# The taps of GpSimd in a depthwise convolution: the multiply as a tensor operation with a broadcast weight

## The chip, the cores and the metric

The kernel runs on one core of a Trainium2 chip. The metric is the device time of one launch in microseconds (us). Three executions of the kernel before are given, and beside them one execution that was profiled.

## The reference

Two layers of a transformer block work on a sequence of 512 latent positions and a context of 256, 1024 channels wide, all in float32. The first layer mixes by neighbourhood attention (8 heads) beside a gated depthwise convolution of 31 taps over 512 channels; the second by a chunked mLSTM. Each layer ends in a SwiGLU. What the change touches is the convolution of the first layer:

```
u, gt = ...                       # two products of h with w_in, 512 channels each
glu = u * sigmoid(gt)
def depthwise_conv(x, w, b):      # w: [31, 512], one weight for each tap and channel
    y = conv(x, w, padding 15 on each side, one group for each channel)
    return y + b
conv_out = silu(layer_norm(depthwise_conv(glu, conv_w, conv_b), ln_g, ln_b))
out = concat([attention, conv_out]) @ w_out
```

## The kernel before, in words

Channels lie on the 128 partitions, positions along the columns. The 512 channels of the convolution are four blocks i = 0 to 3. For each block `glu_out` (L1134) writes the gated input to one of two buffers, `glu0` and `glu1` (block i uses i % 2), with latent and context side by side and zeros between them and around, so that one tap is a shift of the input by one column: a view of SPAN = 798 columns.

The 31 taps of a block are shared out between two engines. VectorE takes the first 18 (DVE_TAPS, `conv_steps` at L1113): one fused multiply and add each (L1120) into its own accumulator `convy[i]`. GpSimd takes the other 13 (POOL_TAPS, `pool_conv` at L378): the first tap is a multiply into `y2` (L388), each later one a multiply into `ptmp` (L392) and an add of `ptmp` to `y2` (L394), each waiting for the one ahead by the semaphore `s_pc`. The weight is one column of `small`, so a value for each partition. That is 13 multiplies and 12 adds for each block, 52 and 48 in all. `merge(i)` (L1127, the operation at L1132) on VectorE waits for both and adds `y2` to `convy[i]`. There is one `y2`, so the first multiply of the next block (L388) waits for the merge of the block ahead (`s_mrg`).

GpSimd also writes masked bias tables for the attention (`masks(hp)`, L352; operations at L367, L369 and L372), one set for each of four head pairs. Its order is written out by hand (L397 to L407): masks(0), block 0, six taps of block 1, masks(1), the rest of block 1, four taps of block 2, masks(2), the rest, four taps of block 3, masks(3), the rest. Much later, in the second layer, it has 16 multiplies at L416, whose two inputs are both broadcast views.

The attention runs in 24 steps U (six for each head pair), and in each of them the four other engines follow orders written out by hand. TensorE: scores (L1668, L1672), transposes of the probabilities (L1686), pieces of the remaining projections (L1643), attend (L1697), small products for the conditioning (L1546, L1553). ScalarE: exponentials (L728), copies of the transposed probabilities (L737). VectorE, for each U: `biased_max(U+1)` (L1162, which waits for the masks by `s_bx`), two or so taps, `normalise(U+1)` (L1178), splits of weights (L430), more taps, and in U = 2, 7, 12 and 18 a merge, then `attn_lo(U)` (L1186), which gates the next transposes. So what stands behind a merge in VectorE's queue is the attention itself.

```
            TAPS_AT = (4, 4) + 16 * (3,)
                conv_steps(taps - min(1 if w_a is not None else 2, taps))
                if U in (2, 7, 12, 18):
                    merge((2, 7, 12, 18).index(U))
```

After the last merge, TensorE sums the four blocks for the layer norm in U = 19 (L1731, L1732, which wait for `s_mrg` 4), the attention steps 19 to 23 end, and the output product of the first layer begins (L1597) at 409.65 us. All that follows (some 1560 us, mostly products at L445) depends on it.

Of the kernel before, what the change touches and what calls it, by code (L numbers as in the profile page):

```python
# [107 lines left out]
def program(nc, A, out):  # L108
    f32, f32r = mybir.dt.float32, mybir.dt.float32r
    ACT, ALU, AX = mybir.ActivationFunctionType, mybir.AluOpType, mybir.AxisListType  # L110
    ctx = ExitStack()
    with ctx:
# [3 lines left out]
        def sem(name):  # L116
            return ctx.enter_context(nc.semaphore(name))
# [27 lines left out]
        def sm(name, i, n=1):  # L145
            return small[:, SM[name][0] + i:SM[name][0] + i + n]
# [4 lines left out]
        def carve(base, at, *shape):  # L151
            n = int(np.prod(shape))
            v = base[:, at:at + n]
            if len(shape) == 2:
                v = v.rearrange("p (a b) -> p a b", a=shape[0])
            if len(shape) == 3:
                v = v.rearrange("p (a b c) -> p a b c", a=shape[0], b=shape[1])
            if len(shape) == 4:
                v = v.rearrange("p (a b c d) -> p a b c d", a=shape[0], b=shape[1], c=shape[2])
            return v, at + n  # L160
# [14 lines left out]
        SPAN = LAT + CTX + 30  # L175
# [3 lines left out]
        y2, at = carve(Xf, at, SPAN)  # L179
        ptmp, at = carve(Xf, at, SPAN)  # L180
# [101 lines left out]
        s_conv, s_pc, s_mrg = sem("conv_step"), sem("pool_conv_step"), sem("conv_merged")  # L282
# [27 lines left out]
        @block.sync  # L310
        def _(sp):
            trig = CN["cos"][0]
            scr_w = scr[:, 0:8192].rearrange("p (a n) -> p a n", a=8)
            sp.dma_start(small[:], A["small"]).then_inc(s_small, 16)
            for i in range(4):
                sp.dma_start(X[:, 2 * i:2 * i + 2], A["xT"][:, 2 * i:2 * i + 2]).then_inc(s_xp[i], 16)
            sp.dma_start(const[:, 0:trig], A["const"][:, 0:trig]).then_inc(s_const, 16)
            for i in range(4):
                if i >= 2:
                    sp.wait_ge(s_adm, 4 * (i - 1))  # L320
                for c in range(2):
                    to = 4 * (i % 2) + 2 * c
                    src = A["ada"][8 * c + 2 * i:8 * c + 2 * i + 2].rearrange("a p n -> p a n")
                    sp.dma_start(scr_w[:, to:to + 2], src).then_inc(s_ada0[i], 16)
                if i == 0:
                    for r in range(2):
                        sp.dma_start(raw[:, r], A["w"][r]).then_inc(s_raw[r], 16)
            sp.dma_start(const[:, trig:NCN], A["const"][:, trig:NCN]).then_inc(s_const, 16)
            for p in range(2, 20):
                sp.wait_ge(s_lo, p - 1)  # L330
                sp.dma_start(raw[:, p % 2], A["w"][AB_ROWS[p]]).then_inc(s_raw[p % 2], 16)
            with sp.Fori(10, NR // 2) as i:
                r = sp.snap(2 * i)
                for j in range(2):
                    src = A["w"][bass.ds(sp.snap(r + j), 1)].rearrange("a p n -> p (a n)")
                    sp.wait_ge(s_lo, r + (j - 1))
                    sp.dma_start(raw[:, j], src).then_inc(s_raw[j], 16)


        @block.gpsimd  # L340
        def _(pool):
            pool.wait_ge(s_h, 8)
            for v in (glu0, glu1, bx0, bx1):
                nc.gpsimd.memset(v, 0.0).then_inc(s_zero, 1)
            for c in range(16):

                src = bass.AP(A["rpb"].tensor, 7 * 384 + 7 * 48 + 15 - c, [[384, 8], [-48, 64], [1, 32]])
                pool.dma_start(braw[8 * c:8 * c + 8].rearrange("p a h k -> p (a h) k"), src).then_inc(s_braw, 16)
            pool.wait_ge(s_braw, 256)
            pool.wait_ge(s_zero, 4)  # L350

            def masks(hp):  # L352

                if hp:
                    pool.wait_ge(s_mx, 8 * hp)
                for h in range(2):
                    H, b = 2 * hp + h, bx[h]
                    for kind, first, k0, k1, kb0, kn, keep in (
                            (0, 256, 8, 16, 8, 8, "low"), (0, 320, 16, 24, 16, 16, None), (0, 320, 24, 32, 16, 16, "high"),
                            (1, 256, 0, 16, 0, 16, "low"), (1, 384, 16, 32, 16, 16, "high"),  # L360
                            (2, 256, 0, 8, 0, 16, "low"), (2, 256, 8, 16, 0, 16, None), (2, 384, 16, 24, 16, 8, "high")):

                        dst = b[:, BX[kind] + first:BX[kind] + first + 8 * kn].rearrange("p (a k) -> p a k", a=8)
                        dst = dst[:, :, k0 - kb0:k1 - kb0]
                        src = braw[:, :, H, k0:k1]
                        if keep is None:
                            i = nc.gpsimd.tensor_copy(dst, src)  # L367
                        elif keep == "low":
                            i = nc.gpsimd.affine_select(out=dst, in_=src, compare_op=ALU.is_ge, fill=-BIG, base=8 * k0 + 7,  # L369
                                                        pattern=[[0, 8], [8, k1 - k0]], channel_multiplier=-1)  # L370
                        else:
                            i = nc.gpsimd.affine_select(out=dst, in_=src, compare_op=ALU.is_ge, fill=-BIG, base=120 - 8 * k0,  # L372
                                                        pattern=[[0, 8], [-8, k1 - k0]], channel_multiplier=1)
                        i.then_inc(s_bx, 1)

            steps = [0]

            def pool_conv(i, j0, j1):  # L378

                src = glus[i % 2]  # L380
                for j in range(j0, j1):
                    tap = DVE_TAPS + j
                    w = sm("conv_w", TAPS * i + tap)
                    if j == 0:
                        pool.wait_ge(s_gf[1], (3, 5, 7, 9)[i])
                        if i:
                            pool.wait_ge(s_mrg, i)
                        nc.gpsimd.tensor_scalar(y2, src[:, tap:tap + SPAN], w, None, ALU.mult).then_inc(s_pc, 1)  # L388
                        steps[0] += 1
                        continue  # L390
                    pool.wait_ge(s_pc, steps[0])
                    nc.gpsimd.tensor_scalar(ptmp, src[:, tap:tap + SPAN], w, None, ALU.mult).then_inc(s_pc, 1)  # L392
                    pool.wait_ge(s_pc, steps[0] + 1)
                    nc.gpsimd.tensor_tensor(y2, y2, ptmp, ALU.add).then_inc(s_pc, 1)  # L394
                    steps[0] += 2

            masks(0)  # L397
            pool_conv(0, 0, POOL_TAPS)
            pool_conv(1, 0, 6)
            masks(1)  # L400
            pool_conv(1, 6, POOL_TAPS)
            pool_conv(2, 0, 4)
            masks(2)
            pool_conv(2, 4, POOL_TAPS)
            pool_conv(3, 0, 4)
            masks(3)
            pool_conv(3, 4, POOL_TAPS)  # L407

            pool.wait_ge(s_g2, GD_END)
            for n in range(16):  # L410
                H, d = n // 2, n % 2
                if n:
                    pool.wait_ge(s_R, n)
                row = nrow[0:48, d, None, :].to_broadcast([48, CH, 128])
                pick = ident[0:48, H:32:8][:, :, None].to_broadcast([48, CH, 128])
                nc.gpsimd.tensor_tensor(rsel[0:48].rearrange("p (c i) -> p c i", c=CH), row, pick, ALU.mult)\  # L416
                    .then_inc(s_rs2, 1)
# [1566 lines left out]
```

## Time and profile before

| | |
|---|---|
| runs | 1965.87, 1968.57, 1973.45 us; median 1968.57 |
| the profiled execution | 1973.65 us, its span 1971.8 us |
| PE busy | 1768.8 us (90% of the span) |
| DVE busy | 844.2 us (43%) |
| ACT busy | 559.9 us (28%) |
| POOL busy | 276.9 us (14%), x204 |
| PE's mean granted clock | 0.921 |

Busy shares are averages over a span in which the stages differ much: GpSimd's work lies nearly all between 59 us and 373 us, in the attention and convolution of the first layer, and in slices 4 to 8 of the 40 (0.2 to 0.4 of a millisecond) it is 90% busy or more. POOL is GpSimd, DVE VectorE, ACT ScalarE, PE TensorE.

### The profile page before, as it was taken

What the parts mean: (1) busy time and instruction counts of PE and PEld (TensorE: products, weight loads), DVE (VectorE), ACT (ScalarE), POOL (GpSimd) and SP (SyncE); (2) the same over time, 40 slices, a digit from 0 to 9 for tenths busy, and PEclk for the clock granted to TensorE, in tenths of its full rate; (3) what the DMA queues carried; (4) which work ended last, traced back from release to release, by engine and by line L of the source; (5) the groups of instructions that cost most, each with busy time, mean ns of one, the idle gap of its engine ahead of it and who ended that gap; (6) DMA issues with size and microseconds to landing.
All of it is one profiled execution on the core that took longest, in us unless ns stands there. A gap on an engine that the chain in (4) does not pass through costs nothing.

```text
span 1971.8 us, 26385 instructions
## 1 busy us (share of the span) xinstructions
PE 1768.8 (90%) x10440; PEld 1459.5 (74%) x10440; DVE 844.2 (43%) x1217; ACT 559.9 (28%) x901; POOL 276.9 (14%) x204
## 2 busy tenths in 40 slices
PE   5989897588999999999999468988989989999997
PEld 4877675367888888888888467666757768787886
DVE  4377686634422222222223525556545443333333
ACT  3334454242321112211222302332333232122131
POOL 0396999500000000000000000000000000000000
PEclk8999898689999999999999759898869999999999
DMA  7623332022113421233215301001002323323333
GB/s 301 76 75 108 101 125 97 1 86 64 44 63 105 148 89 63 59 138 134 63 64 192 120 0 43 22 33 32 22 11 75 128 75 96 95 88 94 96 96 106
DMA packets 47314, 168.99 MB, mean 86 GB/s; under 512 B 5392, under 2 KB 5648, under 8 KB 47120
## 3 DMA queue, kind: packets, MB, share of 16 engines
q1 hardware_dynamic: 31408, 115.47, 18.4%
q10 hardware_dynamic: 15072, 51.53, 7.3%
q0 software_dynamic: 768, 1.08, 0.7%
q8 instruction: 45, 0.74, 0.2%
q14 instruction: 21, 0.17, 0.0%
HBM read 163.83 MB, written 4.19 MB: 85 GB/s over the span
## 4 chain that ended last, share of the span: by engine, by line
PE 78%; DVE 8%; POOL 6%; ACT 3%; issue 2%; DMA 2%; SPq 0%; ACTq 0%; DVEq 0%; POOLq 0%
PE PS L445 57%; PE PS L1643 5%; POOL X L392 3%; PE PS L1537 3%; POOL X L394 2%; PE PS L1546 2%; PE PS L1767 2%; PE PS L1869 2%; DMA scr<-in_ada 2%; PE PS L1868 1%; DVE scr L1416 1%; PE PS L1843 1%; PE PS L1597 1%; DVE w_lo L430 1%; DVE h_lo L963 1%
## 5 line engine op out<-in xcount | busy, mean ns | idle before, releaser
L445 PE MATMUL PS<-h_hi,w_hi 128*128 128x512 f32 (+1 forms) x1296 | 401.0, 364 | 3.7 <-DVE w_lo L430 3.2
L445 PE MATMUL PS<-h_lo,w_hi 128*128 128x512 f32 (+1 forms) x1296 | 394.0, 358 | 0.0
L445 PE MATMUL PS<-h_hi,w_lo 128*128 128x512 f32 (+1 forms) x1296 | 393.8, 358 | 0.0
L430 DVE TENSOR_TENSOR w_lo<-raw,w_hi 128x1024 fp32r<-128x1024 f32 x196 | 240.9, 1231 | 280.3 <-ACT w_hi L425 267.3
L425 ACT ACTIVATE w_hi<-raw 128x1024 fp32r<-128x1024 f32 x196 | 206.2, 1052 | 299.5 <-PE PS L445 244.1
L445 PEld LDWEIGHTS PS<-h_hi,w_hi 128*128 128x128 f32 x1296 | 217.7, 192 | 47.8 <-DVE w_lo L430 5.6
L445 PEld LDWEIGHTS PS<-h_lo,w_hi 128*128 128x128 f32 x1296 | 216.8, 191 | 37.1
L445 PEld LDWEIGHTS PS<-h_hi,w_lo 128*128 128x128 f32 x1296 | 215.5, 190 | 37.3
L445 PE MATMUL PS<-c_hi,w_hi 128*128 128x512 f32 (+1 forms) x688 | 215.9, 367 | 24.7 <-DVE c_lo L1009 18.7
L445 PE MATMUL PS<-c_lo,w_hi 128*128 128x512 f32 (+1 forms) x688 | 213.4, 363 | 0.0
L445 PE MATMUL PS<-c_hi,w_lo 128*128 128x512 f32 (+1 forms) x688 | 212.4, 362 | 0.0
L995 DVE SCALAR_TENSOR_TENSOR X<-PS,mod,X 128x512 f32 (+1 forms) x96 | 60.6, 659 | 279.5 <-PE PS L445 271.5
L416 POOL TENSOR_TENSOR scr<-adaw,const 48x512 f32<-48x512 f32 x16 | 16.7, 1043 | 1069.4 <-DVE adaw L1348 808.3
L445 PEld LDWEIGHTS PS<-c_hi,w_hi 128*128 128x128 f32 x688 | 115.9, 193 | 49.1 <-issue 26.2
L445 PEld LDWEIGHTS PS<-c_hi,w_lo 128*128 128x128 f32 x688 | 116.8, 193 | 20.8
L445 PEld LDWEIGHTS PS<-c_lo,w_hi 128*128 128x128 f32 x688 | 116.5, 193 | 19.9
L392 POOL TENSOR_SCALAR X<-X,small 128x798 f32<-128x798 f32 x48 | 126.7, 2639 | 4.4
L1007 DVE TENSOR_TENSOR scr<-PS,scr 128x768 f32<-128x768 f32 (+1 forms) x44 | 36.3, 824 | 170.8 <-PE PS L445 170.8
L552 ACT ACTIVATE c_hi<-scr 128x768 f32 (+3 forms) x44 | 32.5, 739 | 267.6 <-DVE scr L1007 267.6
L1120 DVE SCALAR_TENSOR_TENSOR c_early<-X,small,c_early 128x798 f32<-128x798 f32 x68 | 97.6, 1436 | 1.1
L549 ACT ACTIVATE scr<-PS 128x768 f32<-128x768 f32 (+1 forms) x44 | 31.1, 706 | 191.8 <-PE PS L445 185.8
L394 POOL TENSOR_TENSOR X<-X 128x798 f32<-128x798 f32 x48 | 83.3, 1736 | 4.0
(259 smaller groups left out, 2055.6 us busy)
## 6 DMA issues: line engine op xcount, KB each, us to landing
raw<-in_w SPq DMA_DIRECT2D x196, 512.0 KB, 3.4
scr<-in_ada ACTq DMA_DIRECT2D x48, 512.0 KB, 5.7
adaw<-in_ada ACTq DMA_DIRECT2D x32, 512.0 KB, 4.3
scr<-in_ada SPq DMA_DIRECT2D x8, 1024.0 KB, 10.6
X<-in_xT SPq DMA_DIRECT2D x4, 768.0 KB, 6.8
X<-in_xT ACTq DMA_DIRECT2D x1, 3072.0 KB, 9.9
x_spill<-X ACTq DMA_DIRECT2D x1, 2048.0 KB, 9.3
X<-x_spill ACTq DMA_DIRECT2D x1, 2048.0 KB, 8.6
```

The source lines that it names most:

```text
L392: nc.gpsimd.tensor_scalar(ptmp, src[:, tap:tap + SPAN], w, None, ALU.mult).then_inc(s_pc, 1)
L394: nc.gpsimd.tensor_tensor(y2, y2, ptmp, ALU.add).then_inc(s_pc, 1)
L425: nc.scalar.activation(w_hi[:, j], raw[:, j].rearrange("p (k n) -> p k n", k=KT), ACT.Copy).then_inc(s_hi, 1)
L430: nc.vector.tensor_tensor(w_lo[:, j], raw[:, j].rearrange("p (k n) -> p k n", k=KT), w_hi[:, j].bitcast(f32), ALU.subtract).then_inc(s_lo, 1)
L445: last = nc.tensor.matmul(G[j][:, a:b], w[:, j, k], m[:, k, a:b], start=(n == 1), stop=(n == 3 * k_tiles))
L995: i = V.scalar_tensor_tensor(out=xs, in0=G[j][:, a:b], scalar=gv, in1=xs, op0=ALU.mult, op1=ALU.add)
L1120: V.scalar_tensor_tensor(out=y, in0=src, scalar=w, in1=y, op0=ALU.mult, op1=ALU.add)\
L1537: last = MM(G[j][:, a:b], x[:, j, k], m[:, k, a:b], start=(k == 0 and n == 0), stop=(k == KT - 1 and n == 2))
L1546: last = MM(PS[g:g + 32, bank, 128 * q:128 * q + 128], sT[:, k], w[:, 128 * k:128 * k + 128], start=(k < 4), stop=(k >= 4))
L1643: last = MM(dst[:, a:b], w[:, p % 2, k], m[:, k, a:b], start=(k == 0 and n == 0), stop=(k == KT - 1 and n == 2))
L1767: last = MM(PS[:, 4, 32 * c:32 * c + 32], x[:, k, 128 * c:128 * c + 128], w[:, k], start=(k == 0 and n == 0), stop=(k == KT - 1 and n == 2))
L1869: last = MM(dst, Pm[:, n % 2, cc], vaug[:, h, c], start=False, stop=True)
```

## The change

The two multiplies of `pool_conv`, at L388 and L392, become tensor operations: the second input is the same column of `small`, now a view that repeats it along 798 columns. The adds, the order, the waits, the masks and the split of taps stay.

```
--- before.py
+++ after.py
@@ -385,11 +385,11 @@
                         pool.wait_ge(s_gf[1], (3, 5, 7, 9)[i])
                         if i:
                             pool.wait_ge(s_mrg, i)
-                        nc.gpsimd.tensor_scalar(y2, src[:, tap:tap + SPAN], w, None, ALU.mult).then_inc(s_pc, 1)
+                        nc.gpsimd.tensor_tensor(y2, src[:, tap:tap + SPAN], w.to_broadcast([128, SPAN]), ALU.mult).then_inc(s_pc, 1)
                         steps[0] += 1
                         continue
                     pool.wait_ge(s_pc, steps[0])
-                    nc.gpsimd.tensor_scalar(ptmp, src[:, tap:tap + SPAN], w, None, ALU.mult).then_inc(s_pc, 1)
+                    nc.gpsimd.tensor_tensor(ptmp, src[:, tap:tap + SPAN], w.to_broadcast([128, SPAN]), ALU.mult).then_inc(s_pc, 1)
                     pool.wait_ge(s_pc, steps[0] + 1)
                     nc.gpsimd.tensor_tensor(y2, y2, ptmp, ALU.add).then_inc(s_pc, 1)
                     steps[0] += 2
```

## Rows read from the trace of the kernel before

**Rows 1.** Profile page, part 4: shares of the chain that ended last, by engine.
```profile
PE 78%; DVE 8%; POOL 6%; ACT 3%; issue 2%; DMA 2%; SPq 0%; ACTq 0%; DVEq 0%; POOLq 0%
```

**Rows 2.** The chain that ended last, 244 to 373 us: start us, us, what.
```profile
244.18 0.99 DVE c_early L1132
245.33 2.30 POOL X L388
...
309.86 2.31 POOL X L388
...
371.22 1.61 POOL X L394
```

**Rows 3.** Groups of instructions by line, GpSimd: busy us, mean ns, idle before.
```profile
L392 POOL TENSOR_SCALAR X<-X,small 128x798 f32<-128x798 f32 x48 | 126.7, 2639 | 4.4
L394 POOL TENSOR_TENSOR X<-X 128x798 f32<-128x798 f32 x48 | 83.3, 1736 | 4.0
...
L388 POOL TENSOR_SCALAR X<-X,small 128x798 f32<-128x798 f32 x4 | 9.2, 2295 | 21.2 <-DVE c_early L1132 21.2
```

**Rows 4.** Single lines: min/median/max ns, first and last start us.
```profile
L392 POOL TENSOR_SCALAR X<-X,small x48: 2284/2359/3959, 107.2 to 368.9; 128x798 f32<-128x798 f32 x48
...
L394 POOL TENSOR_TENSOR X<-X x48: 1595/1608/2392, 109.5 to 371.2; 128x798 f32<-128x798 f32 x48
...
L416 POOL TENSOR_TENSOR scr<-adaw,const x16: 1041/1042/1047, 1181.1 to 1457.9; 48x512 f32<-48x512 f32 x16
```

**Rows 5.** GpSimd's instructions in order of time, 180 to 212 us.
```profile
182.80 2.29 POOL L388 TENSOR_SCALAR X<-X,small 128x798 f32<-128x798 f32 x1 [17.65 <-DVE c_early L1132]
...
207.64 0.29 POOL L369 TENSOR_SCALAR_AFFINE_SELECT scr<-X 128x64 f32<-128x64 f32 x1
...
211.22 0.29 POOL L372 TENSOR_SCALAR_AFFINE_SELECT c_early<-X 128x64 f32<-128x64 f32 x1
```

**Rows 6.** VectorE's instructions in order of time, idle time before them in brackets.
```profile
211.64 0.62 DVE L1162 CUSTOM_DVE_ANT_0 scr<-PS,c_early 128x448 f32<-128x448 f32 x1 [9.22 <-issue]
...
297.96 1.04 DVE L1120 SCALAR_TENSOR_TENSOR c_early<-X,small,c_early 128x798 f32<-128x798 f32 x1
308.69 0.99 DVE L1132 TENSOR_TENSOR c_early<-c_early,X 128x798 f32<-128x798 f32 x1 [9.70 <-POOL X L394]
...
362.33 2.59 DVE L1178 TENSOR_SCALAR scr<-scr 128x512 f32<-128x512 f32 x2
372.93 0.99 DVE L1132 TENSOR_TENSOR c_early<-c_early,X 128x798 f32<-128x798 f32 x1 [8.01 <-POOL X L394]
```

**Rows 7.** TensorE at 215.79 us, with its idle time and releaser.
```profile
215.79 1.12 PE L1697 MATMUL PS<-scr 128*64 128x128 f32 x8 [6.54 <-ACT scr L737]
```

**Rows 8.** Windows, TensorE alone: stretch, length, busy (x), granted clock, DMA share, GB/s.
```profile
215.80:222.40 6.60, 6.60 (x53) 0.50 0.53 193
...
309.80:315.40 5.60, 5.54 (x22) 0.54 0.02 4
```

**Rows 9.** Windows of blocks 1, 2, 3, multiplies of L392 alone: POOL busy (x), clock.
```profile
182.00:244.00 62.00, 31.18 (x12) 0.92 0.33 110
245.00:309.00 64.00, 31.25 (x12) 0.97 0.38 129
309.00:373.00 64.00, 29.83 (x12) 0.74 0.15 50
```

**Rows 10.** The same windows, adds of L394 alone.
```profile
182.00:244.00 62.00, 20.87 (x12) 0.92 0.33 110
245.00:309.00 64.00, 20.47 (x12) 0.97 0.38 129
309.00:373.00 64.00, 20.46 (x12) 0.74 0.15 50
```

**Rows 11.** VectorE's taps at L1120: min/median/max ns, first and last start us.
```profile
L1120 DVE SCALAR_TENSOR_TENSOR c_early<-X,small,c_early x68: 1035/1051/2428, 106.2 to 356.6; 128x798 f32<-128x798 f32 x68
```

More of the change, by code:

```diff
@@ L387, in pool_conv @@
                             pool.wait_ge(s_mrg, i)
-                        nc.gpsimd.tensor_scalar(y2, src[:, tap:tap + SPAN], w, None, ALU.mult).then_inc(s_pc, 1)
+                        nc.gpsimd.tensor_tensor(y2, src[:, tap:tap + SPAN], w.to_broadcast([128, SPAN]), ALU.mult).then_inc(s_pc, 1)
                         steps[0] += 1
@@ L391, in pool_conv @@
                     pool.wait_ge(s_pc, steps[0])
-                    nc.gpsimd.tensor_scalar(ptmp, src[:, tap:tap + SPAN], w, None, ALU.mult).then_inc(s_pc, 1)
+                    nc.gpsimd.tensor_tensor(ptmp, src[:, tap:tap + SPAN], w.to_broadcast([128, SPAN]), ALU.mult).then_inc(s_pc, 1)
                     pool.wait_ge(s_pc, steps[0] + 1)
```

## The prediction

> **What bounds the kernel now.** I read the chain that ended last first, because GpSimd's 14% of the span says nothing about it. The chain gives GpSimd 6% of the span [rows 1], and in order of time this share is one piece: from the merge of block 1 at 244.18 us to the last add at 371.22 us the chain runs almost without a break through GpSimd's multiplies and adds [rows 2]. Ahead of and behind that stretch it runs through TensorE. So the question is what is late there, and what would be late next.
>
> Then VectorE's instructions in order of time, for what waits for GpSimd. There are three such places [rows 6]. (a) `biased_max(6)` at 211.64, idle 9.22 us before it: it waits for masks(1), which GpSimd reaches only after six taps of block 1 and finishes at 211.22 + 0.29 = 211.5 [rows 5]. (b) The merge of block 2 at 308.69: VectorE was ready at 297.96 + 1.04 = 299.0 and waited 9.70. (c) The merge of block 3 at 372.93, ready at 362.33 + 2.59 = 364.9, waited 8.01. The merges of blocks 0 and 1 don't wait; at block 0 it is GpSimd that idles 17.65 us [rows 5].
>
> **What one multiply costs after.** As it is, one takes 2.295 us undisturbed (L388, mean) and 2.639 on average at L392; the add, a tensor operation with the same 798 columns on the same engine, takes 1.736 on average [rows 3], 1.595 at least [rows 4]. The open price is that of a tensor multiply with one input that repeats a single column. The trace has one: L416 multiplies two broadcast views, 512 columns, in 1.042 us, with a spread of 6 ns [rows 4]. That is 2.04 ns a column, against 1.600/798 = 2.00 for the add and 2.295/798 = 2.88 for the scalar form. So neither the multiply nor the zero step costs extra, and I price the new multiply as the add: 798 x 2.04 = 1.62 us undisturbed, and in each stretch the mean of the adds there. L416 runs on 48 partitions only; should the time depend on them the price is open, so the bounds are 1.60 us (the add) below and 3.96 us (the longest multiply now, [rows 4]) above. I take the value near the add, as the same opcode on the same shape.
>
> The trace thus has the two-input form faster than the one-input form, 1.60 against 2.30 us. The Trainium skill, GPSIMD Engine Reference, Engine selection, says the reverse: two-input elementwise operations are about twice as slow as on VectorE because both inputs share one read port, one-input ones run at roughly line rate. By that rule this edit could only lose, and the slower rival below would be the forecast; the trace disagrees with it at the scalar form.
>
> **The sum, wait by wait.** Block 0: 12 multiplies and the first get shorter, some 13 us in all. Worth nothing: the idle time of 17.65 us before block 1 [rows 5] grows instead, since merge(0) comes from VectorE's own order. If that cover were gone it would be 13 us.
>
> (a) Up to masks(1), GpSimd runs L388 (2.29 to about 1.65, saves 0.6) and five multiplies. In block 1 twelve L392 take 31.18 us [rows 9] and twelve adds 20.87 [rows 10], so one multiply saves (31.18 - 20.87)/12 = 0.86, five 4.3. Masks(1) ends 4.9 to 5.1 us earlier, at 206.5. `biased_max(6)` would have been free at about 205.5, so I count 5.1. TensorE's wait of 6.54 us behind it [rows 7] shrinks to about 1.4. That wait also costs a clock: after it the granted clock is 0.50 for 6.6 us [rows 8], so the 1.2 GHz level; the same work at full clock takes half, so 3.2 us more. Steps follow each other by TensorE there, so both count: **8.3 us**.
>
> Block 1: GpSimd saves 12 x 0.86 + 0.7 = 11 us and ends near 232, while VectorE comes to merge(1) at 244.18 - 8.3 = 235.9. It still doesn't wait, and block 2 starts 8.3 us earlier, near 237.0.
>
> (b) Block 2: multiplies 31.25 to 20.47 [rows 9, 10], 10.8, and 0.7 for the first: 11.5. Its last add ends at 308.6 - 8.3 - 11.5 = 288.8. VectorE is ready at 299.0 - 8.3 = 290.7, so the wait is gone and what is late next is the attention itself. merge(2) moves from 308.7 to 290.7, **18.0 us** in all.
>
> (c) Block 3: multiplies 29.83 to 20.46 [rows 9, 10], 9.4, and 0.7: 10.1. GpSimd ends at 372.8 - 18.0 - 10.1 = 344.7. VectorE's own arrival: 364.9 - 18.0 = 346.9, less the low-clock stretch after the wait of (b) (5.6 us at 0.54 [rows 8], so about 2.9) = 344.0. The two are level; merge(3) falls near 344.8 instead of 372.9, **28.1 us** in all.
>
> After merge(3) nothing changes: sums, last steps, output product and the 1560 us behind keep their lengths and shift. The L416 multiplies are untouched. No wait, DMA or buffer is added; the load of X behind merge(3) moves with it. Sum against the profiled execution: 1973.65 - 28.1 = 1945.5. That execution is 5.1 above the median of the runs shown, so the forecast for the median is 1968.57 - 28.1 = **1940.5 us**.
>
> **What is uncertain in it.** GpSimd's and VectorE's instructions slow each other while both run: L392 loses 0.34 us on average (2.639 - 2.295), the adds 0.14 (1.736 - 1.595, [rows 3, 4]), and VectorE's taps, 1.05 us at the median, reach 2.43 [rows 11]. In my sum the new multiply loses as little as an add. If it keeps more, its mean is 2.0 instead of 1.74, 0.26 more each: six before masks(1) 1.6 us; block 2 then ends at 288.8 + 1.6 + 13 x 0.26 = 293.8 where VectorE is ready at 292.3, 1.5; block 3 another 3.4; 6.5 in all, so a gain of 21.6. On the other side, with GpSimd's instructions shorter, VectorE is held for less each time: it could arrive at merge(3) some 3 us sooner and GpSimd too, for a gain of 33.
>
> **The rivals.** *Contention eats part* (chance 0.20): the new multiply is held as often as the old, mean 2.0 us; gain 21.6, so 1947. For it: both inputs now come from SBUF. Against: the adds have two and are held least. *More comes back* (0.17): VectorE's holds shrink, gain 33, 1935.5. *The form was not what cost* (0.04): multiplying takes its 2.3 us in any form, no change, 1968.6. Against: the multiplies at L416. *Slower: the repeated column is fetched in a pass of its own* (0.04). The multiply then takes two passes of the add, 3.2 us, plus 0.3 of holding: 3.5, 0.9 more than now. Masks(1) comes 5.4 later; block 1 ends 13 x 0.9 = 11.7 later, at 254.7, past VectorE's 249.6, so GpSimd then bounds every block: 10.5 + 11.7 + 11.7 = 34 us, 2002.5. It decides from a mean of 2.64 us on. Here too L416 speaks against it, where both inputs repeat. The rule of the Trainium skill named above (GPSIMD Engine Reference, Engine selection) points to this side. The forecast itself has 0.55.
>
> **How the numbers follow.** Something like 0.5% (10 us) is what a measurement of this kernel can tell from no change. The forecast, the contention case and the case of more all lie beyond it: 0.92 faster. Same 0.04, slower 0.04. The range takes in these three cases and the spread of the runs (about 3 below and 5 above the median): 1935.5 less 5 is 1930.5, 1947 plus 5 is 1952.
>
> **What the profile after should show.** L388 and L392 as TENSOR_TENSOR with a minimum near 1.61 us and a mean of 1.7 to 1.8, about 41 us less busy time on GpSimd; masks(1) ending near 206.5 and no low-clock stretch behind it; GpSimd idle some 31 us before block 1 about 5 before block 2 and 3 before block 3; the wait of merge(2) gone or under 1 us; merge(3) near 345 with a wait of 0 to 3 us; the output product beginning near 381.5; lengths behind it unchanged. I am wrong if the minimum of the multiply is not near the add's, if merge(2) still waits several us for L394, or if the stretch behind 409.65 changes its length.

## The result and the profile after

The change made the kernel slower: 1982.10 us median of 20 runs against 1972.92 of 20, ratio 1.0049, 95% interval 1.0038 to 1.0061. The profiled execution took 1980.02 us. I had forecast 1940.5.

The price of the multiply was right, and better than forecast. From the views of single lines of the kernel after (min/median/max ns):

```profile
L392 POOL TENSOR_TENSOR X<-X,small x48: 1507/2138/2580, 111.6 to 370.9; 128x798 f32<-128x798 f32 x48
...
L394 POOL TENSOR_TENSOR X<-X x48: 1595/2222/2662, 113.2 to 372.5; 128x798 f32<-128x798 f32 x48
...
L1120 DVE SCALAR_TENSOR_TENSOR c_early<-X,small,c_early x68: 1032/2184/2434, 106.4 to 372.6; 128x798 f32<-128x798 f32 x68
```

A multiply that nobody disturbs takes 1.51 us, less even than the add. But the medians tell the rest. The add, which was not touched, goes from 1.608 to 2.222 us, and VectorE's tap, not touched either, from 1.051 to 2.184 [rows 4, 11]. The medians have moved from the undisturbed to the disturbed value: each engine now holds up the other in more than half of these instructions. The groups by line on the page after (busy us, mean ns) say what that sums to:

```profile
L1120 DVE SCALAR_TENSOR_TENSOR c_early<-X,small,c_early 128x798 f32<-128x798 f32 x68 | 121.4, 1785 | 1.1
...
L394 POOL TENSOR_TENSOR X<-X 128x798 f32<-128x798 f32 x48 | 97.3, 2027 | 3.8
L392 POOL TENSOR_TENSOR X<-X,small 128x798 f32<-128x798 f32 x48 | 92.9, 1936 | 3.5
```

GpSimd's 96 instructions fall from 210.0 us [rows 3] to 190.2, and its busy time in all from 276.9 to 259.2, so 17.7 us where I had counted on 41. And VectorE pays: its taps take 121.4 us where they took 97.6 (68 at a mean of 1.436), its busy time rises by 38 us to 882.5. The chain that ended last shows who sets the end now (page after, part 4, by engine):

```profile
PE 77%; DVE 13%; ACT 3%; DMA 2%; issue 2%; POOL 1%; SPq 0%; ACTq 0%; DVEq 0%; POOLq 0%
```

GpSimd went from 6% to 1%, VectorE from 8% to 13% [rows 1]. In order of time the places of [rows 5, 6] look so (VectorE, then GpSimd, of the kernel after; idle time before the instruction in brackets):

```profile
189.44 0.98 DVE L1132 TENSOR_TENSOR c_early<-c_early,X 128x798 f32<-128x798 f32 x1
...
250.47 0.98 DVE L1132 TENSOR_TENSOR c_early<-c_early,X 128x798 f32<-128x798 f32 x1
...
312.99 0.98 DVE L1132 TENSOR_TENSOR c_early<-c_early,X 128x798 f32<-128x798 f32 x1
...
379.20 0.98 DVE L1132 TENSOR_TENSOR c_early<-c_early,X 128x798 f32<-128x798 f32 x1
```

```profile
190.57 1.52 POOL L388 TENSOR_TENSOR X<-X,small 128x798 f32<-128x798 f32 x1 [26.00 <-DVE c_early L1132]
251.59 1.52 POOL L388 TENSOR_TENSOR X<-X,small 128x798 f32<-128x798 f32 x1 [5.35 <-DVE c_early L1132]
314.11 1.52 POOL L388 TENSOR_TENSOR X<-X,small 128x798 f32<-128x798 f32 x1 [4.97 <-DVE c_early L1132]
```

No merge waits for GpSimd any more; GpSimd waits for every merge. The merges stand 7.8, 6.3, 4.3 and 6.3 us later than before (181.6, 244.2, 308.7, 372.9). The whole loss is there after block 0; blocks 1 to 3 take 189.8 us against 191.3.

How the two engines interlock is seen in block 0, where VectorE runs several taps in a row. Before, GpSimd has one scalar-form multiply and one tensor add in turn:

```profile
126.83 2.90 POOL L392 TENSOR_SCALAR X<-X,small 128x798 f32<-128x798 f32 x1
129.81 1.94 POOL L394 TENSOR_TENSOR X<-X 128x798 f32<-128x798 f32 x1
```

and VectorE beside it:

```profile
127.61 1.60 DVE L1120 SCALAR_TENSOR_TENSOR c_early<-X,small,c_early 128x798 f32<-128x798 f32 x1
...
129.24 1.05 DVE L1120 SCALAR_TENSOR_TENSOR c_early<-X,small,c_early 128x798 f32<-128x798 f32 x1
...
130.33 2.27 DVE L1120 SCALAR_TENSOR_TENSOR c_early<-X,small,c_early 128x798 f32<-128x798 f32 x1
```

The tap at 127.61 begins and ends inside the scalar-form multiply, at 1.60 us; the next takes its undisturbed 1.05; the one that meets the tensor add takes 2.27 and ends 0.85 us after the add. A pair on GpSimd lasts 5.0 us and three taps go by. After the change:

```profile
129.48 2.14 POOL L392 TENSOR_TENSOR X<-X,small 128x798 f32<-128x798 f32 x1
131.70 2.23 POOL L394 TENSOR_TENSOR X<-X 128x798 f32<-128x798 f32 x1
```

```profile
130.29 2.18 DVE L1120 SCALAR_TENSOR_TENSOR c_early<-X,small,c_early 128x798 f32<-128x798 f32 x1
...
132.50 2.27 DVE L1120 SCALAR_TENSOR_TENSOR c_early<-X,small,c_early 128x798 f32<-128x798 f32 x1
```

One tap for each tensor operation, strictly in turn: a pair lasts 4.5 us and two taps go by. GpSimd's pair is 10% shorter, and VectorE's tap a third longer (2.25 against 1.67 us).

### The profile page after: what moved, and what is told of

It reads as the page before. It is cut to its first block, busy times and chain, and to the rows that moved or that the text cites. A ratio compares the mean times of both kernels' runs of the same rounds, so it can differ in the third digit from the quotient of the medians.

```text
span 1978.2 us, 26385 instructions
## 1 busy us (share of the span) xinstructions
PE 1761.7 (89%) x10440; PEld 1453.8 (73%) x10440; DVE 882.5 (45%) x1217; ACT 560.2 (28%) x901; POOL 259.2 (13%) x204
## 4 chain that ended last, share of the span: by engine, by line
PE 77%; DVE 13%; ACT 3%; DMA 2%; issue 2%; POOL 1%; SPq 0%; ACTq 0%; DVEq 0%; POOLq 0%
PE PS L445 56%; PE PS L1643 5%; DVE c_early L1120 3%; PE PS L1537 3%; DMA scr<-in_ada 2%; PE PS L1546 2%; PE PS L1767 2%; PE PS L1869 2%; PE PS L1868 1%; DVE w_lo L430 1%; DVE scr L1416 1%; PE PS L1843 1%; DVE scr L1178 1%; PE PS L1697 1%; PE PS L1597 1%
## 5 line engine op out<-in xcount | busy, mean ns | idle before, releaser
L430 DVE TENSOR_TENSOR w_lo<-raw,w_hi 128x1024 fp32r<-128x1024 f32 x196 | 246.6, 1260 | 277.3 <-ACT w_hi L425 264.3
L1120 DVE SCALAR_TENSOR_TENSOR c_early<-X,small,c_early 128x798 f32<-128x798 f32 x68 | 121.4, 1785 | 1.1
L394 POOL TENSOR_TENSOR X<-X 128x798 f32<-128x798 f32 x48 | 97.3, 2027 | 3.8
L392 POOL TENSOR_TENSOR X<-X,small 128x798 f32<-128x798 f32 x48 | 92.9, 1936 | 3.5
## 6 DMA issues: line engine op xcount, KB each, us to landing
X<-in_xT ACTq DMA_DIRECT2D x1, 3072.0 KB, 10.1
```

The source lines that it names most:

```text
L392: nc.gpsimd.tensor_tensor(ptmp, src[:, tap:tap + SPAN], w.to_broadcast([128, SPAN]), ALU.mult).then_inc(s_pc, 1)
L430: nc.vector.tensor_tensor(w_lo[:, j], raw[:, j].rearrange("p (k n) -> p k n", k=KT), w_hi[:, j].bitcast(f32), ALU.subtract).then_inc(s_lo, 1)
L1120: V.scalar_tensor_tensor(out=y, in0=src, scalar=w, in1=y, op0=ALU.mult, op1=ALU.add)\
```

## The experiments

Theory H: a GpSimd operation with two inputs in SBUF (the tensor form) holds up a two-input VectorE instruction for nearly all its length, the scalar form for only a part. Rivals: W, that it is the reading of the repeated weight column; R, that a tap waits once for each GpSimd instruction whatever its form, so that shorter ones mean more waits.

### Which property of the operation holds VectorE up

**e1_swap**: the tensor multiply stays, the add becomes a scalar form.

```
-                    nc.gpsimd.tensor_tensor(y2, y2, ptmp, ALU.add).then_inc(s_pc, 1)
+                    nc.gpsimd.tensor_scalar(y2, ptmp, w, None, ALU.mult).then_inc(s_pc, 1)
```

> The multiplies of GpSimd are the tensor form with the repeated weight, as after the change, but its 48 adds are replaced by scalar-form multiplies (y2 = ptmp times weight), so its taps are not summed up. The mix of forms is thus that of before with the roles swapped. Theory H (a GpSimd tensor operation, with two inputs in SBUF, holds up a VectorE tap for all its length, the scalar form for only a part): VectorE's taps at L1120 fall back to the mean of before, 1.4 to 1.5 us, merge of block 0 near 182 us, time within 5 us of before. Rival W (it is the reading of the repeated weight column, next to VectorE's own reads of the weights, that holds VectorE up): taps stay at 1.7 to 1.8 us, merge of block 0 near 189 us.

**e2_full_operand**: the second input of L392 is 798 real columns.

```
-ptmp, src[:, tap:tap + SPAN], w.to_broadcast([128, SPAN]), ALU.mult
+ptmp, src[:, tap:tap + SPAN], src[:, tap:tap + SPAN], ALU.mult
```

> As after the change, but the second input of the 48 multiplies at L392 is the 798-column input itself (a square), not the repeated weight: its taps are left out of the result. Theory H: the same as after the change, taps at L1120 1.7 to 1.8 us on average, the multiply 1.5 to 1.6 us at least and about 1.95 on average, merge of block 0 near 189 us. Rival W: taps back at 1.4 to 1.5 us.

**e3_short_scalar**: the kernel before, L392 cut in length.

```
-nc.gpsimd.tensor_scalar(ptmp, src[:, tap:tap + SPAN], w, None, ALU.mult)
+nc.gpsimd.tensor_scalar(ptmp[:, 0:520], src[:, tap:tap + 520], w, None, ALU.mult)
```

> The kernel before, with the 48 scalar-form multiplies at L392 cut to 520 of 798 columns (the rest is left out of the result): one takes some 1.5 us undisturbed, as long as the tensor form after the change, so GpSimd's instructions come as densely. Theory H: the form decides, so in a pair of multiply and add VectorE still gets more than two taps through; taps at L1120 1.3 to 1.5 us on average, merge of block 0 near 182 us, and merges 2 and 3 come without a wait: 20 to 30 us faster than before. Rival R (a VectorE tap waits once for each GpSimd instruction, whatever its form, so shorter ones mean more waits): taps 1.7 to 1.8 us, merge of block 0 near 189 us, time like after.

**e4_all_scalar**: the kernel before with the edit of e1 to its adds.

> The kernel before with its 48 adds replaced by scalar-form multiplies (GpSimd's taps are not summed up): no tensor operation is left in the taps of GpSimd. Theory H: taps at L1120 fall below before, to 1.2 to 1.35 us on average, the longest (2.4 us before) to 1.7 or less; GpSimd's chain grows by 36 x 0.7 = 25 us beyond block 0, less what its holds shrink, so the whole is some 20 us slower than before. Rival R or W: the taps stay at 1.4 us or more, with some of 2.3 us.

Measured, one run each, beside 1975.52 us for the kernel before on the same chip: e1 1966.67, e2 1978.73, e3 1953.06, e4 1990.05. VectorE's taps, one view of the line for each of e1, e2, e3 and e4 in this order:

```profile
L1120 DVE SCALAR_TENSOR_TENSOR c_early<-X,small,c_early x68: 1035/1052/2307, 106.8 to 352.7; 128x798 f32<-128x798 f32 x68
```

```profile
L1120 DVE SCALAR_TENSOR_TENSOR c_early<-X,small,c_early x68: 1036/2185/2434, 105.7 to 374.0; 128x798 f32<-128x798 f32 x68
```

```profile
L1120 DVE SCALAR_TENSOR_TENSOR c_early<-X,small,c_early x68: 1031/1366/2427, 105.9 to 342.9; 128x798 f32<-128x798 f32 x68
```

```profile
L1120 DVE SCALAR_TENSOR_TENSOR c_early<-X,small,c_early x68: 1035/1050/1790, 106.6 to 360.6; 128x798 f32<-128x798 f32 x68
```

The 20 runs of the kernel before lie between 1965.9 and 1978.7 us, so times of one run each prove little below some 10 us; the traces carry the argument here. e1 was expected within 5 us and came out 8.9 us faster; its merge 3 stands 5.8 us earlier (367.1), which fits its lengths: its tensor multiply is 0.09 us shorter than the tensor add and L388 0.8 us shorter, 1.9 us for each block on GpSimd. e4 lost 14.5 us, not 20. As to what was asked: with e1, in which the repeated weight is still read 48 times, the mean falls to 1.418 us, as before; with e2, in which it is not read at L392, it stays at 1.786. That rules out W from both sides. In e3 GpSimd's instructions came nearly as densely as after (the short multiply 2.2 us beside a busy VectorE, a pair 4.8), and the mean was 1.485; its row of six taps in block 0 takes 9.7 us against 10.1 before and 13.7 after: R is out. Between two tensor adds VectorE gets two more taps through here too, and the one inside the short scalar form takes 1.37 us, not 1.60:

```profile
123.86 2.21 POOL L392 TENSOR_SCALAR X<-X,small 128x520 f32<-128x520 f32 x1
```

```profile
124.65 1.37 DVE L1120 SCALAR_TENSOR_TENSOR c_early<-X,small,c_early 128x798 f32<-128x798 f32 x1
...
126.05 1.05 DVE L1120 SCALAR_TENSOR_TENSOR c_early<-X,small,c_early 128x798 f32<-128x798 f32 x1
```

In e4, with no two-input operation in GpSimd's taps, the longest tap is 1.79 and the mean 1.242. In its block 0 the taps alternate between 1.60 and 1.05 us, two for each scalar form:

```profile
123.58 2.74 POOL L392 TENSOR_SCALAR X<-X,small 128x798 f32<-128x798 f32 x1
126.41 2.62 POOL L394 TENSOR_SCALAR X<-X,small 128x798 f32<-128x798 f32 x1
```

```profile
124.20 1.60 DVE L1120 SCALAR_TENSOR_TENSOR c_early<-X,small,c_early 128x798 f32<-128x798 f32 x1
...
125.83 1.05 DVE L1120 SCALAR_TENSOR_TENSOR c_early<-X,small,c_early 128x798 f32<-128x798 f32 x1
```

So a tap loses 0.55 us to a scalar form of 798 columns, 0.32 to one of 520, and some 1.2 us to a tensor form (2.25 less 1.05). These runs show that the form decides; whether it does so by the number of its inputs, or by how fast it reads and writes, none of them separates. Of e3's forecast one part missed: merge 2 came without a wait, merge 3 still with 2.4 us. Its 22 us are also what a shorter chain on GpSimd is worth when the form stays.

### Where in the kernel it costs

**e5_tensor_block0** and **e6_tensor_blocks123**: at both lines

```
+                    if i == 0:        # e6: if i > 0:
+                        nc.gpsimd.tensor_tensor(ptmp, src[:, tap:tap + SPAN], w.to_broadcast([128, SPAN]), ALU.mult).then_inc(s_pc, 1)
+                    else:
                     nc.gpsimd.tensor_scalar(ptmp, src[:, tap:tap + SPAN], w, None, ALU.mult).then_inc(s_pc, 1)
```

> The change in block 0 alone (13 multiplies); blocks 1 to 3 keep the scalar form. Theory H: in block 0 VectorE is on the path and GpSimd is not, so here the change can only lose: merge of block 0 near 189.5 us instead of 181.6, all behind it as before but later, time 6 to 8 us (0.3 to 0.4%) above before. Rival S (block 0 is covered by GpSimd's idle time of 17.65 us and the loss arises in blocks 1 to 3): within 2 us of before.

> The change in blocks 1 to 3 alone (39 multiplies). Theory H: merge of block 0 at 181.6 as before, from there on the lengths of after: merge 1 near 243, merge 2 near 305, merge 3 near 371 us, without waits for GpSimd; GpSimd's gain is eaten by VectorE's holds there, time within 3 us of before. Rival S: 8 to 10 us slower than before, as the whole change is.

e5: 1983.38 us median, ratio 1.0053 (1.0035 to 1.0072), the whole loss, from 13 multiplies that I had priced at nothing. e6: 1973.41, ratio 0.9999 (0.9986 to 1.0012), nothing won by the other 39. So blocks 1 to 3 neither win nor lose, and the loss arises in block 0. The merges of e6 (at L1138 there, as the edit adds lines) came as expected, and without waits:

```profile
181.94 0.98 DVE L1138 TENSOR_TENSOR c_early<-c_early,X 128x798 f32<-128x798 f32 x1
...
242.95 0.98 DVE L1138 TENSOR_TENSOR c_early<-c_early,X 128x798 f32<-128x798 f32 x1
...
305.41 0.98 DVE L1138 TENSOR_TENSOR c_early<-c_early,X 128x798 f32<-128x798 f32 x1
...
371.71 0.98 DVE L1138 TENSOR_TENSOR c_early<-c_early,X 128x798 f32<-128x798 f32 x1
```

e5's merge 0 stood at 192.5, 3 us later than I expected and 3.1 later than after, and its merge 3 at 384.6, 5.4 later than after; why block 0 took longer there than in the kernel after is not shown. Its expectation speaks of block 0 as if VectorE had been on the path there already; in the kernel before it is TensorE up to 128.5 us (see "Block 0" below).

**e9_no_pool_taps**: `pool_conv` returns at once.

> The kernel before without GpSimd's taps at all (13 of 31 taps left out of the result; the merge adds convy to itself so that VectorE's work stays). It shows the pace of the attention with nothing from GpSimd but the masks. Theory H: taps at L1120 all near 1.05 us; merge 0 near 178, merge 3 near 335 to 340 us, 35 to 40 us faster than before; so that VectorE's holds cost some 30 to 40 us after the change and my forecast, which let VectorE run at least as fast as before, fails there. Rival P (TensorE's own pace of 11 us a step sets merge 3, and holds are covered by it): merge 3 not below 355.

One run: 1939.00 us, 34.4 below the median of before, a little short of the 35 to 40 expected; merges at 177.8, 227.8, 282.1 and 332.0, the last 41 us earlier. The groups by line, VectorE, 100 to 400 us, of this kernel (its lines are one off: L1121 is the tap, L1177 the scaling of the probabilities):

```profile
L1121 DVE SCALAR_TENSOR_TENSOR c_early<-X,small,c_early 128x798 f32<-128x798 f32 x68 | 71.2, 1047 | 1.1
...
L1177 DVE TENSOR_SCALAR scr<-scr 128x448 f32<-128x448 f32 (+2 forms) x48 | 18.8, 434 | 0.9
```

and of the kernel after (this stretch has 44 of its 48 scalings; all 48 have a mean of 1.039 us):

```profile
L1120 DVE SCALAR_TENSOR_TENSOR c_early<-X,small,c_early 128x798 f32<-128x798 f32 x68 | 121.4, 1785 | 1.1
L1178 DVE TENSOR_SCALAR scr<-scr 128x448 f32<-128x448 f32 (+2 forms) x44 | 46.7, 1101 | 0.8
```

Holds cost the taps 121.4 - 71.2 = 50 us after the change, and 97.6 - 71.2 = 26 before. Rival P is out: TensorE's pace would allow merge 3 at 332.

### What to do about it

**e7_masks_first**, the kernel after with

```
+            masks(1)
-            pool_conv(1, 0, 6)
-            masks(1)
-            pool_conv(1, 6, POOL_TAPS)
+            pool_conv(1, 0, POOL_TAPS)
```

> The kernel after, with masks(1) written ahead of block 1's taps, so in GpSimd's idle time of 26 us before merge 0; nothing is left out. Theory H: VectorE no longer waits for the masks near 215 us (3.4 us idle before L1162), and the 5 us of masks leave the stretch; but VectorE bounds the blocks, so 3 to 6 us less than after, about the time of before. Rival G (GpSimd still bounds after the change): merges 1 to 3 all move by the 5 us and more, 8 to 10 us below after.

The wait before `biased_max(6)` went and merge 3 came 4.3 us earlier (374.9), so G is out; but the time was 1982.21 us, ratio to before 1.0034 (1.0014 to 1.0055), where I had expected about 1, and not clear of the 1.0049 of after. Its 12 runs fall in two lots, four at 1972 to 1975 and eight at 1981 to 1988. In the profiled one (1982.27, so of the longer lot) the output product took 16.36 us where that of after took 15.05, at a granted clock of 0.90 and 1.00, and from its start to the end 1566.0 us passed against 1559.2. So in this execution the 4.3 us were lost behind, in work that the edit doesn't touch. That stretch differs between executions without any edit to it: the kernel before has 16.36 us and, to the end, 1562.2 there. Why eight of the twelve runs lie in the longer lot stays open.

**e10_twelve_scalar**, the kernel before with

```
-POOL_TAPS = 13
+POOL_TAPS = 12
-            TAPS_AT = (4, 4) + 16 * (3,)
+            TAPS_AT = (4, 4, 4, 4, 3, 3) + 2 * (3, 3, 3, 3, 3, 4)
```

> The kernel before, scalar form, with one tap of each block moved from GpSimd to VectorE (12 and 19 instead of 13 and 18), nothing left out. If in the kernel before GpSimd bounds blocks 2 and 3 and VectorE's holds come from its tensor adds alone (theory H), each block is 4.6 us shorter on GpSimd and 1.4 us longer on VectorE: merge 2 some 4.5, merge 3 some 8 us earlier than before, time 6 to 9 us below before. Rival V (VectorE bounds there already): no gain, or slower.

1965.30 us, ratio 0.9965 (0.9954 to 0.9977); merges 2 and 3 at 305.8 and 366.8, 2.9 and 6.2 earlier. V is out for the kernel before.

**e11_twelve_masks_first** is e10 with the edit of e7; **e12_eleven_masks_first** has 11 taps besides, with TAPS_AT = 6 * (4,) + 2 * (3, 3, 3, 3, 4, 4).

> As e10, and masks(1) written ahead of block 1's taps, in GpSimd's idle time. Theory H: the 9.2 us wait for masks(1) at 212 us goes, with the low-clock stretch behind it: merge 1 near 237, merge 2 near 298, merge 3 near 358 us, 12 to 16 us below before. Rival V: as e10, within 4 us of it.

> As e11 with 11 taps on GpSimd and 20 on VectorE. Theory H: another 4.6 us less on GpSimd for blocks 2 and 3, and with fewer tensor adds fewer holds; merge 3 near 352 us, 16 to 22 us below before, if VectorE's extra taps (1.4 us each) still fit beside TensorE's steps of 11 us. Rival V: VectorE is now the bound and nothing is won over e11.

e11: 1957.78 us, ratio 0.9934 (0.9916 to 0.9952), merges 1 to 3 at 236.2, 298.7, 357.9. e12: 1952.86 us, ratio 0.9913 (0.9895 to 0.9931), merges at 237.1, 296.5, 355.6, none of them waiting; merge 3 missed my 352 by 3.6. It beats both kernels: GpSimd does less, in the form that lets VectorE through. No merge waits for GpSimd any more, so the next tap moved would have to pay on VectorE; that was not tried. Nor was the tensor form with 11 or 12 taps, so how much of e12's gain is owed to the form is not shown.

**e13_fourteen_tensor**, the other way: e7 with 14 tensor-form taps on GpSimd and 17 on VectorE, TAPS_AT = (4, 4, 3, 3, 2, 2) + 2 * (3, 3, 3, 3, 3, 2).

> The kernel after (tensor form) with masks(1) first and one tap of each block moved from VectorE to GpSimd (14 and 17). Theory H: GpSimd had 5 us of idle time before blocks 2 and 3, so its 3.6 to 4.3 us more nearly fit, and VectorE has one held tap of 2.2 us less for each block: merge 3 some 4 us earlier than e7 (374.9), time about that of before. Rival: GpSimd's tensor operations are so much in the way that the extra one costs VectorE as much as it saves: no change against e7.

1975.44 us, ratio 1.0018 (1.0002 to 1.0035). Merge 3 stands at 375.1, no earlier than e7's 374.9, so on the trace the rival holds: the tap that VectorE no longer does is paid back in holds, and merge 3 waits 1.6 us for GpSimd again. The median is nearer to the kernel before than e7's, which, as e7's runs fall in two lots, proves little.

## Why the prediction was wrong

- **The bound before** was right. GpSimd set merges 2 and 3 and masks(1) (by the page it is 90% busy in slices 5 to 7 alone, 60% in slice 4 and 50% in slice 8); e3 (22 us for a shorter multiply) and e10 (one tap less) show it. The forecast that the multiply would cost as the add was right undisturbed (1.51 us for my 1.62).
- **Its mean** was wrong: 1.936 us where I had 1.74, and the adds went up with it, from 1.736 to 2.027. I took the mean of the adds as a property of the add. It was a property of the mix: in block 0 before, the tap at 129.24 overlaps the add at 129.81 by 0.48 us and the add takes 1.94; after the change the tap at 130.29 overlaps the add at 131.70 by 0.77 and the add takes 2.23.
- **The step that failed** is VectorE's own arrival. "VectorE is ready at 299.0 - 8.3 = 290.7" and "364.9 - 18.0" carried its times over unchanged, and the paragraph on uncertainty went further: "with GpSimd's instructions shorter, VectorE is held for less each time". The runs show the reverse: a tap loses 0.55 us to a scalar form (0.32 to one cut to 520 columns, e3) and 1.2 to the tensor form that takes its place though that is shorter, whatever its second input (e2). VectorE came to merge 3 at 379.2, 35 us later than my 344.0. [rows 11] had the sign in it: a median of 1.05 with a maximum of 2.43 is at least two kinds of tap (there are three: 1.05, 1.60 and 2.27), and I didn't ask which GpSimd instruction stood beside which kind. That was in the trace of before, in the lines of block 0 quoted above.
- **Block 0** I had costed at nothing because GpSimd idles behind it. The cover hid GpSimd's time, not VectorE's. Before, the chain that ended last runs through TensorE up to 128.5 us, and VectorE idles 1.4, 1.9 and 1.9 us for others between 110 and 136 us. The chain of the kernel before, start us, us, what:

```profile
101.72 12.71 PE PS L1643 x72
...
115.72 12.73 PE PS L1643 x72
```

After the change VectorE is the one on the path from 112 to 149 us: it runs 12 taps and five other two-input operations (L430, L1150) there without a break, and most are held longer (the five take 2.3 to 2.6 us each, 1.0 to 1.7 before). The idle time is used up first, the rest is loss. Merge 0 moved by 7.8 us. e5 shows that this alone is the loss, 1.0053.
- **(a), (b), (c)**: the waits of merges 2 and 3 fell from 9.7 and 8.0 us to nothing, as forecast. The wait before `biased_max(6)` fell from 9.2 only to 3.4: masks(1) ended at 217.9, not 206.5. From the first multiply of block 1 to there GpSimd took 27.4 us where it had taken 28.7, so 1.3 us of my 5.1, and a stretch of 6.8 us at a granted clock of 0.50 stayed behind it (from 222.1 us). None of it moved the end, since VectorE came later by as much or more. From merge 1 to merge 3 the chain of before gives GpSimd 116 of 129 us, that of after none: TensorE 69 us and VectorE 47 (sums of the pieces of the chain). This is the rival that I lacked: the engine that had waited becomes the bound by the very change. Of those I had, *contention eats part* had the right kind of cause (mean 2.0 us for the multiply, measured 1.936) but priced GpSimd's side alone, a fifth of what was lost at merge 3 (6.5 us of 34), and the slower rival, a repeated column fetched apart, the right sign and a wrong mechanism (e2).
- **Behind merge 3** I expected no change: 1600.7 us from merge 3 to the end of the profiled execution before, 1600.8 after. Right, but by luck: it is made of 3.0 us more up to the output product and 2.9 less after. One small reading in (c) was off as well: 5.6 us at a clock of 0.54 give back 2.6 us at full clock, not 2.9.

The Trainium skill, SBUF — State Buffer, SBUF: two separate sides, has the rule that bears on this case: of a VectorE instruction with two SBUF inputs and a GpSimd instruction that reads SBUF, the one that starts first has the shared ports for the whole instruction and the other is blocked. For the tensor form the trace nearly agrees (the tap of 2.27 us, 1.05 of it its own, ends 0.85 us after the add). For the scalar form it doesn't: it reads SBUF too, and a tap begins and ends inside one, losing 0.55 us. By the rule as it stands both forms hold VectorE alike, and shorter ones would hold it for less, so it would not have warned of the loss either.

## What to carry to other kernels

An operation's own duration is not its whole price where two engines hold each other up: ask also what it does to the instructions of its neighbour, and read minimum, median and maximum of those, not their mean alone. Before pricing a change of form, find in the trace which instruction of the neighbour stands beside which form. Idle time of the changed engine covers its own time only; if its neighbour is on the path there, or close to it, the slower form that holds the neighbour for less can be the better one (e5), or the engine is given less to do (e12).

## What the runs showed of the hardware that I had not expected

- GpSimd's scalar-form multiply (one input in SBUF, one value for each partition) takes 2.28 us for 798 columns, its tensor form 1.51 with a repeated column or a full second input, the tensor add 1.60.
- A VectorE tap of 1.05 us takes 1.60 beside a scalar form and some 2.2 beside a tensor form, and GpSimd's operations stretch by 0.6 us too (2.28 to 2.9, 1.51 to 2.14, 1.60 to 2.22; the add in block 0 before by 0.34). Both engines lose.
- VectorE's scaling of the probabilities (L1178), with a single SBUF input, is held as well: 0.434 us on average without GpSimd's taps (e9), 0.899 before and 1.039 after the change. What lets a tap pass through a scalar form is not shown by any run here.
